# Attention heads taken in pairs on TensorE, with three score banks, five places of exponentials and one more head in flight

## The chip, the cores and the metric

The kernel runs on one core of one Trainium2 chip. The metric is device time in microseconds for one execution of the whole program. TensorE does the matrix products, VectorE (DVE) and ScalarE (ACT) the elementwise work, GpSimd (POOL) and SyncE (SP) issue transfers. Each engine works through its own list of instructions in order, and waits on semaphores that the others raise.

## The reference

Two layers of a decoder trunk, 256 tokens by 1024 channels, float32. Each layer mixes tokens in three branches with 16 heads in all, then runs a SwiGLU.

```
h   = rms_norm(x) * (1 + scale1) + shift1
A: 8 heads, 96 wide queries and keys, dense causal attention
B: 4 heads, 64 wide, own block of 256 keys, ALiBi
C: 4 heads, 64 wide, the 64 keys with the highest indexer score, ALiBi
p   = softmax(q k^T * scale + mask);  y = p v          (each head)
x   = x + gate1 * ((sum_i sigmoid(g_i) * (y_i @ w_br_i)) @ w_out)
x   = x + gate2 * SwiGLU(rms_norm(x) * (1 + scale2) + shift2)
```

For C the keys are chosen by sixteen rounds of "eight largest, then strike them out" on the indexer's scores.

## The kernel before

Products with weights are done in three passes of a split format: each weight slab of 128 x 2048 is loaded by SP into `raw` (three places), copied by ACT into `w_hi` (function `hi`), and its rest is put by DVE into `w_lo` (function `lo`). `lo_ready` tells TensorE that a slab can be used. A ring of three slabs ties the engines together: `hi` of slab n waits until slab n-3 has been used.

The change lies in the stage of the heads. It has one loop on each engine, over n, and each loop runs past the sixteen heads by a few steps so that the work of several heads overlaps. Heads 0 to 3 are branch B, 4 to 11 branch A, 12 to 15 branch C. Each loop sees a head n at a step of its own:

- TensorE, step n: `scores(n+1)` (two products into bank 4 or 5), `turn_p(n-2)` (three transposes of the probabilities into bank 6 or 7), `weigh_v(n-3)` (probabilities times V into one half of the 128 partitions of bank 2 or 3; two heads fill one bank). At steps 1, 3, 5, 8, 10, 12, 15 and 18 (`GATE_STEPS`) half a slab of gate logits follows, 24 products, `gate_slab`.
- DVE, step n: `scores_max(n)` (mask, maximum over keys, negative maximum), `normalize(n-1)`, on odd n from 5 the remainder `y_lo` of a pair of heads, at n = 5, 10, 14 and 20 a `lo` of a weight slab, then one or two rounds of the key selection up to n = 10, and at n = 11 the mask of branch C. In layer 0 an `ada_next` follows at n = 15 and 17.
- ACT, step n: `expo(n)` (two exponentials), the copy of the transposed head n-2 from PSUM into `pt_sb`, on odd n from 5 the copy `y_hi` of a pair from PSUM, and at n = 4, 9, 13 and 19 a `hi` of a weight slab with the tanh of a finished gate slab behind it (`gate_act`).

A pair's chain is thus: `weigh_v` of both heads on TensorE, `y_hi` on ACT, `y_lo` on DVE. `pt_sb` and the buffers in which a head's probabilities lie (`p_sb`) rotate, the latter over four places. The queries of two heads of B or C lie in the two halves of the partitions of `pq_t`; `kz_t` holds the keys of one head in its half and zeros in the other, so that a score product over all 128 rows takes one head alone.

Behind the loop come the branch projections: `branch` of slab `S_BR` (it needs `y_lo` of the first six pairs), `turn_row` twice, then slab `S_BR + 1`, `S_BR + 2` and `S_BR + 3`. `lo(S_BR)` is the one at n = 14 of the DVE loop, `lo(S_BR + 1)` that at n = 20.

Of the kernel before, what the change touches and what calls it, by code (L numbers as in the profile page):

```python
# [10 lines left out]
ACT = mybir.ActivationFunctionType  # L11
# [177 lines left out]

PAIR_Y = [4, 5, 0, 1, 2, 3, 6, 7]  # L190
# [12 lines left out]
def build(nc, x, c, ada, slabs, vec, gain_rows, const, out):  # L203
    with ExitStack() as ctx:
# [53 lines left out]
        p_sb = [acc[:, 384 * i:384 * (i + 1)] for i in range(4)]  # L258
        pt_sb = [acc[:, 2304 + 384 * i:2304 + 384 * (i + 1)] for i in range(2)]
# [248 lines left out]
        def _(pe):  # L508
# [95 lines left out]
            for l in range(DEPTH):  # L604
# [178 lines left out]
                def scores(n):  # L783
                    kind, h = HEADS[n]
                    if kind == "a":
                        q, k = qk_t[0:A_QK, h, :], qk_t[0:A_QK, A_HEADS + h, :]
                    else:
                        j = (0 if kind == "c" else 1)
                        q, k = pq_t[:, 2 * j + h // 2, :], kz_t[:, 4 * j + h, :]
                    if n == 0:  # L790

                        pe.wait_ge(gate_out.sem, gate_out.at(l, 8))
                    if n >= 2:

                        pe.wait_ge(ttr_done.sem, ttr_done.at(l, 2 * (n - 1)))
                    b = bank[4 + n % 2]
                    nc.tensor.matmul(b[:, 0:P], q[:, 0:P], k[:, 0:P], start=True, stop=True)
                    nc.tensor.matmul(b[:, P:P + T], q[:, P:T], k[:, :], start=True, stop=True).then_inc(scored.sem, 1)

                def turn_p(n):  # L800

                    pe.wait_ge(p_ready.sem, p_ready.at(l, n + 1))
                    if n >= 2:

                        pe.wait_ge(pt_out.sem, pt_out.at(l, n - 1))
                    for j in range(3):
# [4 lines left out]
                def weigh_v(n):
                    kind, h = HEADS[n]
                    at = {"a": P * h + A_NOPE, "b": C_BV + HD * h, "c": C_CV + HD * h}[kind]
                    pair = n // 2
                    if n % 2 == 0 and pair >= 2:

                        pe.wait_ge(y_lo_done.sem, y_lo_done.at(l, pair - 1))
                    pe.wait_ge(pt_out.sem, pt_out.at(l, n + 1))
                    r, y = HD * (n % 2), bank[2 + pair % 2]
                    nc.tensor.matmul(y[r:r + HD, 0:T], proj[:, 0, at:at + HD], pt_sb[n % 2][:, 0:T],  # L820
                                     start=True, stop=False, skip_group_check=True)
                    nc.tensor.matmul(y[r:r + HD, P:T], proj[:, 1, at:at + HD],
                                     pt_sb[n % 2][:, T:T + P], start=False, stop=True,
                                     skip_group_check=True).then_inc(pv_done.sem, 1)

                scores(0)
                for n in range(NH + 3):
                    if n + 1 < NH:
                        scores(n + 1)
                    if 2 <= n <= NH + 1:  # L830
                        turn_p(n - 2)
                    if n >= 3:
                        weigh_v(n - 3)
                    if n in GATE_STEPS:
                        half = GATE_STEPS.index(n)
                        gate_slab(l, 8 + half // 2, (half % 2,))

                for hf in range(2):
                    banks = BR_BANKS[hf]

                    def branch(slot, b0, base, k0, n_k):
                        hi, lo = [y_hi[:, k0 + k, :] for k in range(n_k)], [y_lo[:, k0 + k, :] for k in range(n_k)]
                        return channel_slab(slot, [(bank[b0 + m // 2][:, (m % 2) * T:(m % 2 + 1) * T], m * P,
                                                    [base + 512 * k for k in range(n_k)], hi, lo, m % 2 == 0)
                                                   for m in range(4)], True, True)

                    s = S_BR + 2 * hf

                    pe.wait_ge(y_lo_done.sem, y_lo_done.at(l, (B_HEADS + A_HEADS) // 2))
                    if hf:  # L850
                        pe.wait_ge(row_out.sem, row_out.at(l, 2))
                    slot = slab(l, s)
                    branch(slot, banks[0], 0, 0, 4).then_inc(slab_used.sem, 1)
# [112 lines left out]
        def _(act):  # L966
# [88 lines left out]
            for l in range(DEPTH):  # L1055
# [164 lines left out]
                def expo(n):  # L1220
# [3 lines left out]
                    for t, (c0, c1) in enumerate(((0, P), (P, P + T))):  # L1224
                        nc.scalar.activation(p_sb[n % 4][:, c0:c1], p_sb[n % 4][:, c0:c1], ACT.Exp,  # L1225
# [3 lines left out]
                for n in range(NH + 4):  # L1229
                    if n < NH:  # L1230
                        expo(n)
                    if 2 <= n <= NH + 1:
                        act.wait_ge(p_tp.sem, p_tp.at(l, n - 1))
                        if n >= 4:

                            act.wait_ge(pv_done.sem, pv_done.at(l, n - 3))
                        nc.scalar.activation(pt_sb[n % 2], bank[6 + n % 2][:, 0:P + T], ACT.Copy)\
                            .then_inc(pt_out.sem, 1)
                    if n >= 5 and n % 2:
                        pair = (n - 5) // 2  # L1240
                        act.wait_ge(pv_done.sem, pv_done.at(l, 2 * pair + 2))
                        nc.scalar.activation(y_hi[:, PAIR_Y[pair], :], bank[2 + pair % 2][:, 0:T],
                                             ACT.Copy).then_inc(y_hi_done.sem, 1)
# [85 lines left out]
        def _(dve):  # L1329
# [115 lines left out]
            for l in range(DEPTH):  # L1445
# [203 lines left out]
                def scores_max(n):  # L1649
# [4 lines left out]
                    if n >= 4:  # L1654

                        dve.wait_ge(p_tp.sem, p_tp.at(l, n - 3))
                    for t, (c0, c1) in enumerate(((0, P), (P, P + T))):
                        nc.vector.tensor_tensor_reduce(p_sb[n % 4][:, c0:c1], bank[4 + n % 2][:, c0:c1], mask[:, c0:c1],  # L1658
# [6 lines left out]
                def normalize(n):  # L1665
                    dve.wait_ge(exped.sem, exped.at(l, 2 * n + 2))
                    link(nc.vector.reciprocal(rinv[n % 2], rowsum[n % 2]))
                    for t, (c0, c1) in enumerate(((0, P), (P, P + T))):
                        ins = nc.vector.tensor_scalar(p_sb[n % 4][:, c0:c1], p_sb[n % 4][:, c0:c1],
# [3 lines left out]
                for n in range(NH + 5):  # L1673
# [4 lines left out]
                    if 5 <= n < NH + 4 and n % 2:  # L1678
                        pair = (n - 5) // 2
                        dve.wait_ge(y_hi_done.sem, y_hi_done.at(l, pair + 1))  # L1680
                        nc.vector.tensor_tensor(y_lo[:, PAIR_Y[pair], :], bank[2 + pair % 2][:, 0:T],
# [187 lines left out]
```

## Time and profile before

| | us |
|---|---|
| median of 3 runs | 949.47 (948.67 to 950.23) |
| the profiled execution | 948.36 |
| its span, first to last instruction | 946.3 |
| TensorE busy | 900.5 (95%), 5020 instructions |
| DVE busy | 701.9 (74%) |
| ACT busy | 497.6 (53%) |
| mean granted TensorE clock | 0.991 |

TensorE is busy for 95% of the span, but its ends are modelled and its instructions overlap, so the share alone doesn't say that it sets the time of every stage. The stage of the heads runs from about 182 to 246 us in layer 0 and from about 644 to 706 us in layer 1. In the rows an fp32 product stands as two instructions (x2); L797 and L798 are the scores, L807 the transposes, L820 and L822 `weigh_v`, L529 to L531 the products of weight slabs; L1658 and L1662 are `scores_max`, L1667 and L1669 `normalize`, L1681 `y_lo`, L1343 `lo`, L1225 `expo`, L1237 the copy into `pt_sb`, L1242 `y_hi`, L982 `hi`, L1037 `gate_act`.

### The profile page before, as it was taken

Reading aid. Unit: us, or ns where it says so; the run is one execution under the profiler, and the core shown is the slowest. Engines: PE = TensorE matmul, PEld = TensorE weight load, DVE = VectorE, ACT = ScalarE, POOL = GpSimd, SP = SyncE. Lnnn points to the kernel's source line nnn. Section 1 sums busy time; section 2 is a strip of 40 time slices with the busy share of each in tenths; the row PEclk is TensorE's granted clock in tenths of the full one; section 3 lists DMA queues with packets and bytes.
Section 4 is the critical chain, followed back from the end, with each engine's and each line's share of the span. In section 5 each row is a group of like instructions: output and inputs, shape, how many; then the busy total and the mean of one; then the engine's idle time right before and its main releaser. Section 6 shows DMA issues by size and latency. Waiting matters only on the chain.

```text
span 946.3 us, 12773 instructions
## 1 busy us (share of the span) xinstructions
PE 900.5 (95%) x5020; PEld 767.1 (81%) x5020; DVE 701.9 (74%) x1119; ACT 497.6 (53%) x718; POOL 27.7 (3%) x51
## 2 busy tenths in 40 slices
PE   8998988999999999999989998899899999999998
PEld 6788978977887888888868997898689778888886
DVE  5988899787797767586579967987867966575454
ACT  5554965356448443443473469474454664343441
POOL 0010000000000000000001000000000000000000
PEclk9999989999999999999999999999999999999999
DMA  9979723414743857777538973251245456554451
GB/s 377 412 288 398 269 95 134 178 45 169 277 145 145 314 204 271 297 269 277 212 134 330 379 250 142 99 196 63 89 161 195 181 182 220 218 184 184 166 178 45
DMA packets 29582, 198.12 MB, mean 209 GB/s; under 512 B 3282, under 2 KB 3794, under 8 KB 7507
## 3 DMA queue, kind: packets, MB, share of 16 engines
q1 hardware_dynamic: 23474, 155.22, 43.9%
q0 software_dynamic: 5760, 41.95, 11.7%
q8 instruction: 40, 0.66, 0.3%
q10 hardware_dynamic: 288, 0.14, 0.1%
q14 instruction: 20, 0.16, 0.0%
HBM read 196.24 MB, written 1.05 MB: 208 GB/s over the span
## 4 chain that ended last, share of the span: by engine, by line
PE 51%; DVE 31%; ACT 9%; DMA 6%; issue 4%; DVEq 0%; ACTq 0%
PE bank L568 12%; PE bank L570 12%; PE bank L569 12%; DVE w_lo L1343 10%; DMA raw<-in_slabs_dram 5%; PE bank L529 4%; PE bank L531 3%; PE bank L530 3%; ACT w_hi L982 3%; DVE score L1528 2%; DVE front L1350 2%; DVE acc L1658 2%; DVE acc L1350 1%; DVE score L1585 1%; PE bank L917 1%
## 5 line engine op out<-in xcount | busy, mean ns | idle before, releaser
L1343 DVE TENSOR_TENSOR w_lo<-raw,w_hi 128x2048 fp32r<-128x2048 f32 (+2 forms) x146 | 316.5, 2172 | 139.0 <-ACT w_hi L982 137.5
L982 ACT ACTIVATE w_hi<-raw 128x2048 fp32r<-128x2048 f32 (+2 forms) x146 | 264.3, 1811 | 150.7 <-PE bank L570 92.4
L568 PE MATMUL bank<-w_hi,h_hi 128*128 128x512 f32 x536 | 211.3, 394 | 8.2 <-DVE w_lo L1343 5.1
L570 PE MATMUL bank<-w_lo,h_hi 128*128 128x512 f32 x536 | 209.2, 390 | 0.0
L569 PE MATMUL bank<-w_hi,h_lo 128*128 128x512 f32 x536 | 208.9, 390 | 0.0
L568 PEld LDWEIGHTS bank<-w_hi,h_hi 128*128 128x128 f32 x536 | 100.6, 188 | 34.3 <-DVE w_lo L1343 7.7
L529 PE MATMUL bank<-h_hi,w_hi 128*128 128x256 f32 x384 | 113.2, 295 | 10.0 <-DVE w_lo L1343 10.0
L570 PEld LDWEIGHTS bank<-w_lo,h_hi 128*128 128x128 f32 x536 | 100.6, 188 | 21.3
L569 PEld LDWEIGHTS bank<-w_hi,h_lo 128*128 128x128 f32 x536 | 100.7, 188 | 20.1
L530 PE MATMUL bank<-h_lo,w_hi 128*128 128x256 f32 x384 | 110.0, 286 | 0.0
L531 PE MATMUL bank<-h_hi,w_lo 128*128 128x256 f32 x384 | 109.9, 286 | 0.0
L529 PEld LDWEIGHTS bank<-h_hi,w_hi 128*128 128x128 f32 x384 | 74.9, 195 | 14.5 <-DVE w_lo L1343 9.0
L1350 DVE CUSTOM_DVE_ANT_0 front<-front,cond,cols 128x1024 f32<-128x1024 f32 x68 | 84.4, 1279 | 1.9 <-DMA front<-in_ada_dram 1.7
L530 PEld LDWEIGHTS bank<-h_lo,w_hi 128*128 128x128 f32 x384 | 74.9, 195 | 0.1
L531 PEld LDWEIGHTS bank<-h_hi,w_lo 128*128 128x128 f32 x384 | 74.9, 195 | 0.0
L568 PE MATMUL bank<-w_hi,y_hi 128*128 128x512 f32 x176 | 71.3, 405 | 0.0
L569 PE MATMUL bank<-w_hi,y_lo 128*128 128x512 f32 x176 | 69.5, 395 | 0.0
L570 PE MATMUL bank<-w_lo,y_hi 128*128 128x512 f32 x176 | 69.4, 394 | 0.0
L1287 ACT ACTIVATE proj<-bank 128x256 f32<-128x256 f32 x44 | 16.9, 383 | 76.3 <-PE bank L570 76.2
L1225 ACT ACTIVATE acc<-acc,small 128x128 f32<-128x128 f32 x64 | 28.6, 449 | 47.1 <-DVE small L1662 47.1
L570 PEld LDWEIGHTS bank<-w_lo,y_hi 128*128 128x128 f32 x176 | 33.2, 189 | 7.8
L569 PEld LDWEIGHTS bank<-w_hi,y_lo 128*128 128x128 f32 x176 | 33.3, 189 | 6.8
(204 smaller groups left out, 1321.9 us busy)
## 6 DMA issues: line engine op xcount, KB each, us to landing
raw<-in_slabs_dram SPq DMA_DIRECT2D x124, 1024.0 KB, 4.9
front<-in_ada_dram POOLq DMA_DIRECT2D x29, 1024.0 KB, 6.6
acc<-in_ada_dram POOLq DMA_DIRECT2D x11, 1024.0 KB, 8.1
raw<-in_slabs_dram SPq DMA_DIRECT2D x16, 552.0 KB, 7.8
front<-in_ada_dram SPq DMA_DIRECT2D x5, 1024.0 KB, 10.7
raw<-in_slabs_dram SPq DMA_DIRECT2D x6, 768.0 KB, 6.1
proj<-in_ada_dram SPq DMA_DIRECT2D x2, 1024.0 KB, 8.8
x_t<-in_x_dram SPq DMA_DIRECT2D x2, 512.0 KB, 4.4
```

Of the source, the lines that this page charges most:

```text
L529: nc.tensor.matmul(b_out, st_hi, mv_hi, start=start, stop=False, skip_group_check=True)
L530: nc.tensor.matmul(b_out, st_hi, mv_lo, start=False, stop=False, skip_group_check=True)
L531: return nc.tensor.matmul(b_out, st_lo, mv_hi, start=False, stop=stop, skip_group_check=True)
L568: nc.tensor.matmul(o, hh, wh, start=first, stop=False)
L569: nc.tensor.matmul(o, hl, wh, start=False, stop=False)
L570: return nc.tensor.matmul(o, hh, wl, start=False, stop=final)
L982: nc.scalar.activation(w_hi[:, n % RING, 0:w], raw[:, n % RING, 0:w], ACT.Copy).then_inc(hi_ready.sem, 1)
L1225: nc.scalar.activation(p_sb[n % 4][:, c0:c1], p_sb[n % 4][:, c0:c1], ACT.Exp, bias=negmax[n % 2][:, t:t + 1], scale=slope, accum_out=rowsu ...
L1343: nc.vector.tensor_tensor(w_lo[:, n % RING, 0:w], raw[:, n % RING, 0:w], w_hi[:, n % RING, 0:w], ALU.subtract).then_inc(lo_ready.sem, 1)
L1350: ins = nc.vector.tensor_tensor_reduce(w, w, cond[:], 1.0, cols[:, l, col:col + 1], ALU.mult, ALU.add, mod[:, l, col:col + 1])
L1528: ins = nc.vector.scalar_tensor_tensor(out=score[:, c0:c1], in0=relu_b[h % 4][:, c0:c1], scalar=wt, in1=score[:, c0:c1], op0=ALU.mult, op1 ...
L1658: nc.vector.tensor_tensor_reduce(p_sb[n % 4][:, c0:c1], bank[4 + n % 2][:, c0:c1], mask[:, c0:c1], 1.0, NEG, ALU.add, ALU.max, rowmax[n % ...
```

## The change

It touches the stage of the heads on all three engines.

- The scores of B and C are computed for two heads together, `scores_pair`: head e takes 64 rows of `pq_t` and of `kz_t`, and the products of the two heads follow one another in turn into two banks. Those of A stay single.
- Three banks take the scores (4, 5, 3) rather than two; bank 2 alone takes the weighted V.
- `weigh_v` handles a pair: head 0 into partitions 0 to 63, head 1 into 64 to 127, in turn. It stands at odd steps, and waits for `y_lo` of the pair before.
- `p_sb` has five places and `pt_sb` three. `turn_p`, and the copy into `pt_sb`, see head n-3 at step n. `y_hi` and `y_lo` of a pair move from odd steps from 5 to even steps from 6.
- The wait for the last gate tanh moves from the first scores to the first `weigh_v`.
- `branch` of slab `S_BR` moves into the loop, to step 18, behind the gate slab; the last pair's `weigh_v` stands at step 19, behind it.

The core of the diff:

```diff
+SC_BANKS = (4, 5, 3)
-        p_sb = [acc[:, 384 * i:384 * (i + 1)] for i in range(4)]
-        pt_sb = [acc[:, 2304 + 384 * i:2304 + 384 * (i + 1)] for i in range(2)]
+        p_sb = [acc[:, 384 * i:384 * (i + 1)] for i in range(5)]
+        pt_sb = [acc[:, 1920 + 384 * i:1920 + 384 * (i + 1)] for i in range(3)]
...
+                def scores_pair(n):
+                    kind, h = HEADS[n]
+                    if n >= 2:
+                        pe.wait_ge(ttr_done.sem, ttr_done.at(l, 2 * (n - 1)))
+                    j = 0 if kind == "c" else 1
+                    q = pq_t[:, 2 * j + h // 2, :]
+                    at = [slice(HD * e, HD * (e + 1)) for e in range(2)]
+                    b = [bank[SC_BANKS[(n + e) % 3]] for e in range(2)]
+                    for e in range(2):
+                        nc.tensor.matmul(b[e][:, 0:P], q[at[e], 0:P], kz_t[at[e], 4 * j + h + e, 0:P], start=True, stop=True)
+                    for e in range(2):
+                        nc.tensor.matmul(b[e][:, P:P + T], q[at[e], P:T], kz_t[at[e], 4 * j + h + e, :], start=True,
+                                         stop=True).then_inc(scored.sem, 1)
...
+                def weigh_v(pair):
+                    if pair:
+                        pe.wait_ge(y_lo_done.sem, y_lo_done.at(l, pair))
+                    else:
+                        pe.wait_ge(gate_out.sem, gate_out.at(l, 8))
+                    pe.wait_ge(pt_out.sem, pt_out.at(l, 2 * pair + 2))
...
+                    for e in range(2):
+                        nc.tensor.matmul(bank[2][HD * e:HD * (e + 1), 0:T], proj[:, 0, at[e]:at[e] + HD],
+                                         pt_sb[(2 * pair + e) % 3][:, 0:T],
+                                         start=True, stop=False, skip_group_check=True)
+                    for e in range(2):
+                        nc.tensor.matmul(bank[2][HD * e:HD * (e + 1), P:T], proj[:, 1, at[e]:at[e] + HD],
+                                         pt_sb[(2 * pair + e) % 3][:, T:T + P], start=False, stop=True,
+                                         skip_group_check=True).then_inc(pv_done.sem, 1)
...
+                scores_pair(0)
+                for n in range(NH + 4):
                     if n + 1 < NH:
-                        scores(n + 1)
-                    if 2 <= n <= NH + 1:
-                        turn_p(n - 2)
-                    if n >= 3:
-                        weigh_v(n - 3)
+                        if HEADS[n + 1][0] == "a":
+                            scores(n + 1)
+                        elif n % 2:
+                            scores_pair(n + 1)
+                    if 3 <= n <= NH + 2:
+                        turn_p(n - 3)
+                    if n >= 5 and n % 2:
+                        weigh_v((n - 5) // 2)
                     if n in GATE_STEPS:
                         half = GATE_STEPS.index(n)
                         gate_slab(l, 8 + half // 2, (half % 2,))
+                    if n == NH + 2:
+                        first_branch(0)
...
-                for n in range(NH + 4):
+                for n in range(NH + 5):
                     if n < NH:
                         expo(n)
-                    if 2 <= n <= NH + 1:
-                        act.wait_ge(p_tp.sem, p_tp.at(l, n - 1))
-                        if n >= 4:
-                            act.wait_ge(pv_done.sem, pv_done.at(l, n - 3))
-                        nc.scalar.activation(pt_sb[n % 2], bank[6 + n % 2][:, 0:P + T], ACT.Copy)\
+                    if 3 <= n <= NH + 2:
+                        m = n - 3
+                        act.wait_ge(p_tp.sem, p_tp.at(l, m + 1))
+                        if m >= 3:
+                            act.wait_ge(pv_done.sem, pv_done.at(l, m - 2))
+                        nc.scalar.activation(pt_sb[m % 3], bank[6 + m % 2][:, 0:P + T], ACT.Copy)\
                             .then_inc(pt_out.sem, 1)
-                    if n >= 5 and n % 2:
-                        pair = (n - 5) // 2
+                    if n >= 6 and n % 2 == 0:
+                        pair = (n - 6) // 2
                         act.wait_ge(pv_done.sem, pv_done.at(l, 2 * pair + 2))
...
-                    if 5 <= n < NH + 4 and n % 2:
-                        pair = (n - 5) // 2
+                    if n >= 6 and n % 2 == 0:
+                        pair = (n - 6) // 2
                         dve.wait_ge(y_hi_done.sem, y_hi_done.at(l, pair + 1))
```

## Rows read from the trace of the kernel before

**Rows 1.** Windows, layer 0's stage: length, busy PE, PEld, DVE, ACT, POOL, clock, DMA.
```profile
182.00:246.00 64.00, 57.97 (x387) 46.95 (x388) 51.87 (x198) 35.09 (x98) 2.62 (x5) 1.00 0.30 109
```

**Rows 2.** Waits, 182 to 262 us: total us, times, longest.
```profile
DVE y_lo L1681 <- ACT y_hi L1242: 8.1, 7, 1.4
```

**Rows 3.** Timeline of DVE, step 9: start us, duration us, engine, line.
```profile
212.37 0.29 DVE L1658 CUSTOM_DVE_ANT_0 acc<-bank,konst 128x128 f32<-128x128 f32 x1
...
213.04 0.17 DVE L1662 TENSOR_SCALAR small<-small 128x2 f32<-128x2 f32 x1
...
214.91 0.42 DVE L1681 TENSOR_TENSOR y_lo<-bank,y_hi 128x256 fp32r<-128x256 f32 x1 [1.05 <-ACT y_hi L1242]
215.25 0.42 DVE L1584 MAX8 small<-score 128x8 f32<-128x256 f32 x1
...
216.23 0.29 DVE L1658 CUSTOM_DVE_ANT_0 acc<-bank,konst 128x128 f32<-128x128 f32 x1
```

**Rows 4.** Timeline of ACT, steps 9 and 10.
```profile
213.25 0.40 ACT L1225 ACTIVATE acc<-acc,small 128x128 f32<-128x128 f32 x1 [1.03 <-DVE small L1662]
...
214.51 0.37 ACT L1242 ACTIVATE y_hi<-bank 128x256 fp32r<-128x256 f32 x1
214.77 1.91 ACT L982 ACTIVATE w_hi<-raw 128x2048 fp32r<-128x2048 f32 x1
...
217.11 0.40 ACT L1225 ACTIVATE acc<-acc,small 128x128 f32<-128x128 f32 x1
```

**Rows 5.** Timeline of DVE, steps 12 to 16.
```profile
224.68 0.29 DVE L1658 CUSTOM_DVE_ANT_0 acc<-bank,sel_nd 128x128 f32<-128x128 f32 x1
...
226.09 0.28 DVE L1658 CUSTOM_DVE_ANT_0 acc<-bank,sel_nd 128x128 f32<-128x128 f32 x1
...
230.66 2.29 DVE L1343 TENSOR_TENSOR w_lo<-raw,w_hi 128x2048 fp32r<-128x2048 f32 x1
...
232.87 0.28 DVE L1658 CUSTOM_DVE_ANT_0 acc<-bank,sel_nd 128x128 f32<-128x128 f32 x1
...
235.75 1.27 DVE L1350 CUSTOM_DVE_ANT_0 front<-front,cond,cols 128x1024 f32<-128x1024 f32 x1
...
238.16 0.16 DVE L1667 RECIPROCAL small<-small 128x2 f32<-128x2 f32 x1
```

**Rows 6.** Timeline, the stage's first scores and their first reader.
```profile
182.51 0.46 PE L797 MATMUL bank<-kz_t,front 128*128 128x128 f32 x2 [0.78 <-ACT front L1037]
...
183.44 0.29 DVE L1658 CUSTOM_DVE_ANT_0 acc<-bank,konst 128x128 f32<-128x128 f32 x1 [3.25 <-PE bank L798]
```

**Rows 7.** Timeline of PE, the stage's end in layer 0, and `turn_p(15)` in layer 1.
```profile
238.96 0.55 PE L807 MATMUL bank<-konst,acc 128*128 128x128 f32 x3 [1.42 <-DVE acc L1669]
...
240.09 0.65 PE L820 MATMUL bank<-acc,proj 128*64 128x256 f32 x2
...
240.88 0.39 PE L529 MATMUL bank<-h_hi,w_hi 128*128 128x256 f32 x1
...
249.55 1.04 PE L561 MATMUL bank<-konst,row 128*128 128x128 f32 x8
250.34 0.37 PE L529 MATMUL bank<-y_hi,w_hi 128*128 128x256 f32 x1
...
699.14 0.55 PE L807 MATMUL bank<-konst,acc 128*128 128x128 f32 x3
```

**Rows 8.** Timeline of PE, the indexer's products on four row quarters.
```profile
111.57 0.61 PE L735 MATMUL bank<-row,front 32*128 32x256 f32 x8
```

**Rows 9.** Timeline, then windows of PE: length, busy, clock, DMA share, GB/s.
```profile
151.44 0.39 PE L529 MATMUL bank<-h_hi,w_hi 128*128 128x256 f32 x1 [2.27 <-DVE w_lo L1343]
...
153.00:154.00 1.00, 1.00 (x6) 0.50 0.77 311
...
118.00:142.00 24.00, 20.46 (x132) 0.86 0.28 99
142.00:166.00 24.00, 20.12 (x155) 0.93 0.37 132
```

More of the change, by code:

```diff
@@ L807, in turn_p @@
                         last = nc.tensor.transpose(bank[6 + n % 2][:, j * P:(j + 1) * P],
-                                                   p_sb[n % 4][:, j * P:(j + 1) * P], ident)
+                                                   p_sb[n % 5][:, j * P:(j + 1) * P], ident)
                     last.then_inc(p_tp.sem, 1)
[L811 to L824, printed above, removed]
@@ L826, in _ @@
-                scores(0)
-                for n in range(NH + 3):
-                    if n + 1 < NH:
-                        scores(n + 1)
-                    if 2 <= n <= NH + 1:
-                        turn_p(n - 2)
-                    if n >= 3:
-                        weigh_v(n - 3)
+                def weigh_v(pair):
[4 more added lines that the diff above has]
+                    pe.wait_ge(pt_out.sem, pt_out.at(l, 2 * pair + 2))
+                    at = []
+                    for n in (2 * pair, 2 * pair + 1):
+                        kind, h = HEADS[n]
+                        at.append({"a": P * h + A_NOPE, "b": C_BV + HD * h, "c": C_CV + HD * h}[kind])
+                    for e in range(2):
[6 more added lines that the diff above has]
+                                         skip_group_check=True).then_inc(pv_done.sem, 1)
@@ new lines, in branch, with first_branch @@
+                def branch(slot, b0, base, k0, n_k):
+                    hi, lo = [y_hi[:, k0 + k, :] for k in range(n_k)], [y_lo[:, k0 + k, :] for k in range(n_k)]
+                    return channel_slab(slot, [(bank[b0 + m // 2][:, (m % 2) * T:(m % 2 + 1) * T], m * P,
+                                                [base + 512 * k for k in range(n_k)], hi, lo, m % 2 == 0)
+                                               for m in range(4)], True, True)
+                def first_branch(hf):
+                    pe.wait_ge(y_lo_done.sem, y_lo_done.at(l, (B_HEADS + A_HEADS) // 2))
+                    slot = slab(l, S_BR + 2 * hf)
+                    branch(slot, BR_BANKS[hf][0], 0, 0, 4).then_inc(slab_used.sem, 1)
@@ L836, in _ @@
                         gate_slab(l, 8 + half // 2, (half % 2,))
+                    if n == NH + 2:
+                        first_branch(0)
                 for hf in range(2):
                     banks = BR_BANKS[hf]
[L841 to L845, printed above, removed]
                     s = S_BR + 2 * hf
-                    pe.wait_ge(y_lo_done.sem, y_lo_done.at(l, (B_HEADS + A_HEADS) // 2))
                     if hf:
                         pe.wait_ge(row_out.sem, row_out.at(l, 2))
-                    slot = slab(l, s)
-                    branch(slot, banks[0], 0, 0, 4).then_inc(slab_used.sem, 1)
+                        first_branch(1)
                     if hf == 0:
```

32 lines of the change are left out of this document (14 added, 18 removed).

## The prediction

> **What bounds the kernel now.** The page shows TensorE busy for 95% of the span, so at first sight any TensorE work that is saved is time that is saved. The view that decides is that of the stage of the heads. Its window [rows 1] has TensorE busy 57.97 of 64 us and DVE 51.87 of 64. I then read the waits. DVE waits once for scores, at the stage's start [rows 6], and after that for nothing but `y_hi`, 7 times and 8.1 us in all [rows 2]. DVE's timeline is otherwise without a gap from 183.44 to 243 us, and the same in layer 1 up to the last `normalize`. TensorE has some 6 us of gaps in the same stretch, which end with a release by DVE or ACT; the one at 238.96 is such [rows 7]. So in this stage DVE and ACT together set the pace and TensorE follows, nearly full.
>
> The wait of DVE has a form that one step shows [rows 3, 4]. The negative maximum starts at 213.04, ACT's exponentials of the same head at 213.25, its copy into `pt_sb` follows, `y_hi` starts at 214.51, and DVE's `y_lo` at 214.91. That is 1.87 us after the maximum and 1.66 us after the exponentials' start; DVE has only about 0.73 us of its own work to put between (`scores_max` and `normalize` take 1.41 us together, 224.68 to 226.09 [rows 5], 0.68 of which lie ahead of the maximum). `y_lo` itself takes 0.34 (214.91 to 215.25). One `y_lo` thus costs DVE 1.48 us, and it is ACT's order that sets it, not TensorE. Behind the stage TensorE runs without a gap through the branches, so a delay at the stage's end counts in full.
>
> **The change part by part.** I number times on layer 0's clock; layer 1 starts its stage at 645.12 instead of 183.44, 461.68 later, and repeats it.
>
> *TensorE's saving.* A head's `weigh_v` takes 0.79 us (240.09 to 240.88), two of them with the transposes ahead 1.92 (238.96 to 240.88) [rows 7]. Whether halves run side by side, only a near row can say: on row quarters eight instructions of 256 columns took 0.61 us [rows 8], no longer than the two of one `weigh_v`, 0.65 [rows 7]. I take it that halves do so too. A pair's `weigh_v` then costs 0.79 instead of 1.45 (0.66 saved, eight times a layer), and a pair of scores 0.65 less (four times a layer): 7.9 us of TensorE a layer. The other end is nothing saved. The Trainium skill, TensorEngine Tiling (Array Packing), Theoretical Speedup, gives up to 2 times where a dimension is at most 64, which is the saving that I take; the same page, Key Properties, says that a change of tiling mode drains the engine, and it would put more such changes around the paired scores. By either rule only TensorE's slack changes. As DVE never waits for scores in the body, I count this saving at nothing there. It counts in the last two `weigh_v`, which are on the path below.
>
> *The start.* The first scores wait 0.78 us for the tanh of the last gate [rows 6]; that wait moves to the first `weigh_v`, which comes 13 us later. DVE starts 0.83 earlier, at 182.61: gain 0.83 a layer.
>
> *`y_lo` on even steps.* Up to step 9 there are two of them as before, and one with a longer wait of 0.15 becomes a usual one: step 9 of DVE starts at 211.37 instead of 212.37. Now ACT's order matters. At step 9 ACT does expo, copy, then `hi` and the tanh, 2.34 us (214.77 to 217.11 [rows 4]). Before, `y_hi` stood ahead of `hi` in that step. Now it is in step 10, behind it. ACT: expo(9) starts 212.25, expo and copy take 1.26, `hi` and tanh 2.34, expo(10) starts 215.85, so `y_lo` at 215.85 + 1.66 = 217.51. DVE would have been there at 213.75 + 1.41 = 215.16. With `y_lo` 0.34, `lo` 2.21 (230.66 to 232.87 [rows 5]) and a round of selection 0.98 (215.25 to 216.23 [rows 3]), step 11 starts at 221.04.
>
> Step 11 has no `y_lo` now and the mask of C in place of a round of the same length: 3.86 (212.37 to 216.23 [rows 3]) less 1.48, so step 12 starts at 223.42. It was 224.68 [rows 5] with one `y_lo` more behind it; with that 1.48 added we are at 224.9, the 0.83 gone and 0.2 more. Step 12 has a `y_lo` (1.41 + 1.48 = 2.89 with its wait): step 13 at 226.3. Step 13 is 1.41: step 14 at 227.7. ACT: expo(13) 227.17, 1.26 for it and the copy, `hi` and tanh 2.34, expo(14) starts at 230.8, `y_lo` at 232.4. DVE is ready at 229.1, so it stands for 3.3 us; before, this step had no such wait. Then `y_lo` and `lo`: step 15 starts at 234.95, where it started at 232.87 before [rows 5]. This is 2.1 us later than before, 2.9 later than without the two hold-ups.
>
> *A new wait, TensorE for bank 2.* `weigh_v(pair)` waits for `y_lo` of the pair before. Queued behind it are a gate half or the next scores. In the body TensorE has the room (DVE's next scores were issued ahead of it), but its stalls grow: before pair 5 it stands with 0.45 us of transposes between 227.5 and 232.9.
>
> *The end of the stage.* Layer 0: step 15 of DVE ends at 236.36, `ada_next` takes 2.41 (235.75 to 238.16 [rows 5]), `normalize(15)` 0.65, `y_lo` of pair 5 0.34: 239.76. `weigh_v` of pair 6 can't start before (239.85), and `turn_p(15)` stands behind it. Before, `turn_p(15)` started at 238.96, so 0.89 later. In layer 1, without `ada_next`, ACT's two copies and `y_hi` give `y_lo` of pair 5 at 237.86 and `weigh_v` at 238.3; before 699.14 - 461.68 = 237.46, 0.84 later. From there to the first product of slab `S_BR + 1` took 11.38 us (238.96 to 250.34 [rows 7]).
>
> Now: `weigh_v` 0.79, transposes 0.45, gate half and first branch 8.67 (240.88 to 249.55), `weigh_v` of pair 7 0.79, and then the **new chain**. `lo(S_BR + 1)` is in DVE's step 20, behind `y_lo` of pair 7, which waits for `y_hi`, which waits for the `weigh_v` that now comes after the branch. Before, that `lo` was done some 4.6 us ahead of its use. Now it is V's end + 0.11 + 0.40 (`y_hi` to `y_lo`) + 0.34 + 2.21 + 0.05 = 3.1 us, of which `turn_row` covers 0.79 (249.55 to 250.34): TensorE stands for 2.3 us. Sum 13.8 against 11.38: 2.4 later. Together 3.3 in layer 0 and 3.3 in layer 1. The slabs behind it have room: `S_BR + 2` and `S_BR + 3` follow in DVE at once, and their products are due 5.7 us and more later. POOL's waits for the last `weigh_v` let its transfers start some 10 us later, and SP's load of the first `S_OUT` slab some 8 us later; their readers come over 10 us behind, so I count them at nothing, at most 2 us.
>
> *The clock.* An idle stretch of 2.27 us before 151.44 was followed by a granted clock of 0.50 (1.2 instead of 2.4 GHz) from 153 to 154; over 24 us the mean was 0.93, so 24 x 0.07 = 1.7 us were lost [rows 9]. The two other idle stretches of such a length in the trace were followed by the low level too (one of them lies from 118 to 142 us, mean 0.86, 3.4 us lost [rows 9]); those before 238.96 and before `scores`, of 1.4 us and less, were not. The new stall of 2.3 us ahead of `S_BR + 1` is like the first: 1.7 a layer, all on the path. The near-idle stretch before pair 5 costs 1.7 on the gate half that follows: in layer 0 DVE's `ada_next` covers all but 0.15, in layer 1 it delays `turn_p(13)`, ACT's copy, `y_hi` and the bank by 1.7. The bounds are 0 and 3.4 for each. The Trainium skill, TensorE: Matmul & The Clock Gate, says as well that the default state is throttled and that activity releases it; the trace agrees.
>
> *Sum.* Layer 0: 3.3 + 1.7 + 0.15 = 5.2. Layer 1: 3.3 + 1.7 + 1.7 = 6.7. Together **11.8 us slower** (rounded), 948.36 + 11.8 = 960.2 for the profiled execution. That one lies 1.1 below the median of the runs, so the median is forecast at 949.47 + 11.8 = 961.3.
>
> **The rivals.** *The clock stays up.* Then only the chains count, 2 x 3.3 = 6.6: 956.1. Against it stand three idle stretches of this length out of three. *Halves don't run side by side.* The two `weigh_v` on the path cost 1.45 each: 4 x 0.66 = 2.6 more, 963.9. *ACT's hold-ups at steps 10 and 14 do not come about* (`y_hi` isn't reached late, or DVE has other slack). The pace gains 2.9 a layer: 2 x 0.4 = 0.8, and with the clock 3.4 more: 953.7. *TensorE is the bound after all.* The place is the whole stage; the price is 7.9 us saved and 0.83 at the start a layer, against 2.3 for `S_BR + 1`: 2 x 6.4 = 12.8 **faster**, 936.7. It decides from the point at which DVE would be seen to wait for scores; for it speaks the 95%, against it that this wait occurs once a layer. *It does nothing that shows:* the gains at the start and the stall at the end cancel, 949.5.
>
> **How the numbers follow.** Forecast 0.50; clock stays up 0.19; not side by side 0.11; no hold-ups 0.08 (slower still, as 953.7); TensorE bound 0.07; nothing 0.05. The first three hold 0.80. With the bounds of the clock (5 us down, and up by 1.7 for one more drop, with 2.6) the range is 955.0 to 966.0. A measurement of this kernel tells 0.2%, 1.9 us, from no change. Faster 0.07, same 0.05, slower 0.88.
>
> **What would show it.** Right: DVE's waits for `y_hi` include one of over 2 us at step 10, one of over 3 at step 14 and one of some 8 for the last pair; ACT's `w_hi` and tanh stand between two exponentials ahead of it; TensorE waits about 2.3 us for `w_lo` at the first product behind `turn_row`, and for `y_lo` before `weigh_v`; PEclk falls below 1 in the slices of both stages. Scores and `weigh_v` pairs take about half. Wrong: DVE waiting for scores inside the stage, or `lo(S_BR + 1)` done before `turn_row`, would throw the sum over.

## The result and the profile after

| | before | after |
|---|---|---|
| median, us | 949.17 (948.67 to 950.23, 4 runs) | 961.87 (960.78 to 963.63, 4 runs) |
| the profiled execution | 948.36 | 962.44 |
| its span | 946.3 | 960.4 |
| TensorE busy | 900.5 (95%) | 889.7 (93%) |
| DVE busy | 701.9 | 701.7 |
| mean granted TensorE clock | 0.991 | 0.978 |

The ratio after to before is 1.0134 [1.0116, 1.0152]: the kernel with heads in pairs is 1.3% slower. The forecast was 961.3, from 955.0 to 966.0. TensorE does 10.8 us less and the program takes 12.7 us more.

The lines of the code have moved: L793 and L794 are now the single scores, L806 and L808 those of a pair, L818 the transposes, L835 and L839 `weigh_v`, L532 to L534 the products of slabs, L564 `turn_row`, L1684 and L1688 `scores_max`, L1707 `y_lo`, L1369 `lo`, L1250 `expo`, L1268 `y_hi`, L1007 `hi`, L1062 `gate_act`.

The page of the kernel after, its head and its line of the clock by slices:

```profile
span 960.4 us, 12775 instructions
...
PEclk9999999998999999999999999999989999999999
```

Waits of the kernel after, 182 to 270 us (us in total, times, longest), beside [rows 2]:

```profile
DVE y_lo L1707 <- ACT y_hi L1268: 17.7, 7, 8.5
...
PE bank L835 <- DVE y_lo L1707: 8.2, 6, 3.6
ACT w_hi L1007 <- DMA raw<-in_slabs_dram: 7.9, 1, 7.9
...
PE bank L532 <- DVE w_lo L1369: 2.1, 1, 2.1
```

DVE waits for `y_hi` as often as before and more than twice as long. Two rows are new: TensorE waits for `y_lo` before `weigh_v`, and once for a `w_lo`.

Window of layer 0's stage after (length, busy PE, PEld, DVE, ACT, POOL, clock, DMA), beside [rows 1]:

```profile
182.00:246.00 64.00, 49.86 (x371) 42.54 (x370) 49.21 (x196) 33.43 (x96) 1.05 (x2) 0.92 0.25 94
```

TensorE is busy for 8.1 us less of the same 64 us, and its clock is 0.92 where it was 1.00. DVE's busy time is 2.7 us less: both engines stand more. The stage is longer now, so the same 64 us hold a little less of it (371 instructions of TensorE instead of 387).

Timeline of DVE after, the `y_lo` of steps 10 and 14, the next head's maximum, then the last `y_lo` and the `lo` behind it:

```profile
218.01 0.42 DVE L1707 TENSOR_TENSOR y_lo<-bank,y_hi 128x256 fp32r<-128x256 f32 x1 [2.19 <-ACT y_hi L1268]
...
232.88 0.42 DVE L1707 TENSOR_TENSOR y_lo<-bank,y_hi 128x256 fp32r<-128x256 f32 x1 [3.17 <-ACT y_hi L1268]
...
235.42 0.28 DVE L1684 CUSTOM_DVE_ANT_0 acc<-bank,sel_nd 128x128 f32<-128x128 f32 x1
...
252.30 0.42 DVE L1707 TENSOR_TENSOR y_lo<-bank,y_hi 128x256 fp32r<-128x256 f32 x1 [8.52 <-ACT y_hi L1268]
252.64 4.48 DVE L1369 TENSOR_TENSOR w_lo<-raw,w_hi 128x2048 fp32r<-128x2048 f32 x2
```

Timeline of ACT after, in front of the second of these:

```profile
228.57 0.47 ACT L1263 ACTIVATE acc<-bank 128x384 f32<-128x384 f32 x1
228.95 1.90 ACT L1007 ACTIVATE w_hi<-raw 128x2048 fp32r<-128x2048 f32 x1
230.75 0.58 ACT L1062 ACTIVATE front<-bank 128x512 f32<-128x512 f32 x1
231.22 0.39 ACT L1250 ACTIVATE acc<-acc,small 128x128 f32<-128x128 f32 x1
...
232.47 0.37 ACT L1268 ACTIVATE y_hi<-bank 128x256 fp32r<-128x256 f32 x1
```

`w_hi` (1.90) and the tanh (0.58) lie between two heads' exponentials, and `y_hi` comes behind them. DVE has stood since 229.71 for it.

Timeline of PE after, from before pair 5 to slab `S_BR + 1`, beside [rows 7]:

```profile
233.35 1.12 PE L835 MATMUL bank<-acc,proj 128*64 128x256 f32 x4 [3.65 <-DVE y_lo L1707]
...
241.09 0.65 PE L835 MATMUL bank<-acc,proj 128*64 128x256 f32 x4 [0.99 <-DVE y_lo L1707]
241.57 0.39 PE L839 MATMUL bank<-acc,proj 128*64 128x128 f32 x4
241.89 0.55 PE L818 MATMUL bank<-konst,acc 128*128 128x128 f32 x3
...
251.74 1.09 PE L564 MATMUL bank<-konst,row 128*128 128x128 f32 x8
254.97 0.38 PE L532 MATMUL bank<-y_hi,w_hi 128*128 128x256 f32 x1 [2.14 <-DVE w_lo L1369]
```

The same stretch in windows of PE (length, busy PE, clock, DMA share, GB/s):

```profile
230.00:233.00 3.00, 0.00 (x0) 0.73 0.00 0
233.00:236.00 3.00, 2.65 (x13) 0.50 0.01 3
236.00:239.00 3.00, 3.00 (x19) 0.63 0.83 265
251.00:254.00 3.00, 1.83 (x17) 1.00 0.21 33
254.00:257.00 3.00, 2.02 (x10) 0.71 0.94 388
257.00:260.00 3.00, 3.00 (x21) 0.72 0.98 412
260.00:263.00 3.00, 3.00 (x28) 1.00 1.02 431
```

The clock is low from within the idle stretch of 3.65 us on, and low behind the one of 2.14 us, and the work behind both runs on it. Layer 1 differs before pair 5: there the clock falls ahead of the long stretch, which starts at 698.48, behind two waits of 1.91 and 0.92 us, and stays low for 9 us and more:

```profile
692.00:695.00 3.00, 1.41 (x11) 1.00 0.38 161
696.00:705.00 9.00, 5.66 (x28) 0.50 0.05 7
```

### The profile page after: what moved, and what is told of

Same layout as the page of the kernel before. It is cut to its first block, busy times and chain, and to the rows that moved or that the text cites. A ratio compares the mean times of both kernels' runs of the same rounds, so it can differ in the third digit from the quotient of the medians.

```text
span 960.4 us, 12775 instructions
## 1 busy us (share of the span) xinstructions
PE 889.7 (93%) x5020; PEld 761.9 (79%) x5020; DVE 701.7 (73%) x1119; ACT 497.2 (52%) x718; POOL 27.5 (3%) x51
## 3 DMA queue, kind: packets, MB, share of 16 engines
HBM read 196.24 MB, written 1.05 MB: 205 GB/s over the span
## 4 chain that ended last, share of the span: by engine, by line
PE 50%; DVE 31%; ACT 9%; DMA 5%; issue 4%; DVEq 0%; ACTq 0%
PE bank L571 12%; PE bank L573 12%; PE bank L572 12%; DVE w_lo L1369 11%; DMA raw<-in_slabs_dram 5%; PE bank L532 4%; PE bank L533 4%; PE bank L534 4%; DVE score L1554 2%; ACT w_hi L1007 2%; DVE front L1376 2%; DVE acc L1684 2%; DVE score L1611 1%; ACT acc L1250 1%; PE bank L942 1%
## 5 line engine op out<-in xcount | busy, mean ns | idle before, releaser
L1369 DVE TENSOR_TENSOR w_lo<-raw,w_hi 128x2048 fp32r<-128x2048 f32 (+2 forms) x146 | 316.2, 2172 | 130.0 <-ACT w_hi L1007 128.4
L1007 ACT ACTIVATE w_hi<-raw 128x2048 fp32r<-128x2048 f32 (+2 forms) x146 | 264.0, 1810 | 150.9 <-PE bank L573 92.6
L532 PE MATMUL bank<-h_hi,w_hi 128*128 128x256 f32 x384 | 115.5, 301 | 14.3 <-DVE w_lo L1369 14.3
L533 PE MATMUL bank<-h_lo,w_hi 128*128 128x256 f32 x384 | 112.3, 292 | 0.0
L534 PE MATMUL bank<-h_hi,w_lo 128*128 128x256 f32 x384 | 111.9, 292 | 0.0
L532 PEld LDWEIGHTS bank<-h_hi,w_hi 128*128 128x128 f32 x384 | 77.4, 202 | 18.7 <-DVE w_lo L1369 11.4
L533 PEld LDWEIGHTS bank<-h_lo,w_hi 128*128 128x128 f32 x384 | 77.5, 202 | 0.0
L534 PEld LDWEIGHTS bank<-h_hi,w_lo 128*128 128x128 f32 x384 | 77.3, 201 | 0.0
L1250 ACT ACTIVATE acc<-acc,small 128x128 f32<-128x128 f32 x64 | 28.6, 447 | 52.5 <-DVE small L1688 52.5
L532 PE MATMUL bank<-y_hi,w_hi 128*128 128x256 f32 x128 | 37.8, 295 | 4.3 <-DVE w_lo L1369 4.3
## 6 DMA issues: line engine op xcount, KB each, us to landing
front<-in_ada_dram SPq DMA_DIRECT2D x5, 1024.0 KB, 10.8
```

Of the source, the lines that this page charges most:

```text
L532: nc.tensor.matmul(b_out, st_hi, mv_hi, start=start, stop=False, skip_group_check=True)
L533: nc.tensor.matmul(b_out, st_hi, mv_lo, start=False, stop=False, skip_group_check=True)
L534: return nc.tensor.matmul(b_out, st_lo, mv_hi, start=False, stop=stop, skip_group_check=True)
L1007: nc.scalar.activation(w_hi[:, n % RING, 0:w], raw[:, n % RING, 0:w], ACT.Copy).then_inc(hi_ready.sem, 1)
L1250: nc.scalar.activation(p_sb[n % 5][:, c0:c1], p_sb[n % 5][:, c0:c1], ACT.Exp, bias=negmax[n % 2][:, t:t + 1], scale=slope, accum_out=rowsu ...
L1369: nc.vector.tensor_tensor(w_lo[:, n % RING, 0:w], raw[:, n % RING, 0:w], w_hi[:, n % RING, 0:w], ALU.subtract).then_inc(lo_ready.sem, 1)
```

## The experiments

My theory was that of the forecast: the order of ACT and DVE sets the stage's pace, the late `lo(S_BR + 1)` its end, and each standstill costs a drop of the clock besides. The rivals were a TensorE bound and a clock that doesn't matter. For each kernel I read four points in each layer, in us: from DVE's first `scores_max` to that of step 15 (step 15), and to the first product of slab `S_BR + 1` (`S_BR + 1`); from there to the first product of `w_out` (rest); and from the last tanh ahead of the stage to that product (whole). What whole has over the other two together is the start, from the tanh to the first `scores_max`.

The first point needs care. In e2_hi_behind, e4_both, e8_both_br2 and e9_ylo_after_max `lo(S_BR)`, 2.2 us of DVE, stands behind the `scores_max` of step 15, and in the others ahead of it. In e9_ylo_after_max a `y_lo` more stands behind it as well. So 2.2 us of what these four gain at step 15 is only that move; what the pace gains is seen from `S_BR + 1` on.

| kernel | layer 0: step 15, `S_BR + 1`, rest, whole | layer 1 |
|---|---|---|
| before | 49.43, 66.90, 17.36, 85.93 | 49.43, 65.40, 17.36, 84.43 |
| after | 52.28, 71.83, 18.89, 91.57 | 52.29, 71.51, 18.80, 91.16 |
| e1_lo_last | 52.26, 69.78, 18.53, 89.16 | 52.27, 69.52, 18.54, 88.91 |
| e3_fill | 52.27, 71.78, 17.38, 90.01 | 52.26, 71.91, 17.36, 90.12 |
| e2_hi_behind | 47.24, 69.59, 18.89, 89.33 | 46.79, 68.34, 18.90, 88.09 |
| e4_both | 46.79, 65.53, 18.51, 84.89 | 46.79, 65.51, 18.54, 84.90 |
| e7_lo_all | 48.29, 66.89, 18.54, 86.28 | 48.28, 67.01, 18.54, 86.40 |
| e5_tanh_wait | 49.43, 66.91, 17.36, 84.93 | 49.44, 65.41, 17.35, 83.41 |
| e6_two_passes | 50.22, 66.73, 17.35, 85.75 | 49.20, 64.75, 17.36, 83.78 |
| e8_both_br2 | 46.82, 66.04, 17.36, 84.25 | 47.13, 64.35, 17.35, 82.55 |
| e9_ylo_after_max | 41.39, 63.08, 17.36, 81.29 | 43.87, 62.57, 17.35, 80.76 |
| e10_before_ylo | 47.08, 63.43, 17.35, 81.43 | 47.07, 63.06, 17.35, 81.07 |

### e1_lo_last: the late `lo` alone

```diff
 # DVE, step 20, kernel after
+                    if n == 20:
+                        lo(l, S_BR + 1)
                     if n >= 6 and n % 2 == 0:
                         ... y_lo of the pair
-                    if n - 2 in GATE_AT:
+                    if n - 2 in GATE_AT and n < 20:
                         ... lo
```

> The changed kernel with one move: in DVE's step 20 the remainder of slab S_BR + 1 (lo) is made ahead of y_lo of the last pair, not behind it. Theory (the tail's new chain V, y_hi, y_lo, lo holds TensorE for 2.1 us a layer, and the idle stretch brings the low clock, 1.7 us more): TensorE's wait behind turn_row vanishes, the clock stays up there, 2 x 3.8 = 7.7 us faster than the changed kernel, about 954.2. Rival (the wait is a symptom, the slab would be late anyway through its hi or its transfer): the wait stays, 961.9. Rival on the clock (the stall costs only itself): 2 x 2.1 = 4.3 faster, 957.6.

Measured: 956.54 (956.08 to 958.17), ratio to before 1.008 [1.0065, 1.0095], 5.3 less than after. Slab `S_BR + 1` comes 2.05 and 1.99 us sooner, and the clock in the window from 246 to 275 us rose from 0.94 to 1.00. But the rest fell only from 18.8 to 18.5, as a wait took the place of the low clock. Waits of this kernel from 182 to 275 us:

```profile
PE bank L532 <- DVE proj L1750: 1.1, 1, 1.1
```

L1750 adds up the three branches' results, into `proj`: DVE is now late with that. The stall and its drop of the clock go together here, and a part of what they give back is used up by what is late next. The time lies between the two values expected, 954.2 and 957.6.

### e3_fill: the idle stretch filled, the wait left

Five products, whose result in bank 6 nobody reads, run while TensorE would stand.

```diff
                             turn_row(l, 0, half, bank[half])
+                        for _ in range(5):
+                            nc.tensor.matmul(bank[6][:, 0:T], kz_t[:, 0, 0:P], kz_t[:, 0, :], start=True, stop=True)
```

> The changed kernel with five products of 256 columns, whose result nobody reads, put on TensorE behind turn_row in the place of the 2.1 us in which it stands for w_lo of slab S_BR + 1. The chain to w_lo is untouched. Theory (the idle stretch brings the clock down and that costs 1.7 us a layer by itself): the first product of the slab starts as late as now, within 0.2 us, but the clock stays at its upper level behind it, 3.4 us faster, about 958.5. Rival (the low clock comes from elsewhere or costs nothing on the path): 961.9, or a little more.

Measured: 958.97 (957.02 to 963.19), 1.0108 [1.0079, 1.0137]. Timeline of PE:

```profile
254.82 2.32 PE L885 MATMUL bank<-kz_t 128*128 128x256 f32 x10
257.13 0.39 PE L532 MATMUL bank<-y_hi,w_hi 128*128 128x256 f32 x1
257.36 0.28 PE L533 MATMUL bank<-y_lo,w_hi 128*128 128x256 f32 x1
257.48 0.28 PE L534 MATMUL bank<-y_hi,w_lo 128*128 128x256 f32 x1
```

The slab starts as late as in after, but its products then start 0.12 us apart, where after has 0.21 behind this stall. The rest is 17.38 and 17.36, which is before's 17.36; so the drop of the clock cost 1.5 us in layer 0 and 1.4 in layer 1. The median fell by 2.9, with an interval of some 3 us to either side. The load of the first `w_out` slab, for which ACT waits 8.8 us here (7.9 in after), costs nothing of the rest.

### e2_hi_behind: `hi` and tanh behind `y_hi`

```diff
-                    if n - 1 in GATE_AT:
-                        hi(l, gate_slab_no(GATE_AT[n - 1]) + 2)
-                        gate_act(l, GATE_AT[n - 1])
+                    if n in HI_STEPS:            # {4: 8, 10: 9, 14: 10, 19: 11}, behind y_hi
+                        hi(l, gate_slab_no(HI_STEPS[n]) + 2)
+                        gate_act(l, HI_STEPS[n])
```

DVE's `lo` stands one step behind each.

> The changed kernel with ACT's hi and tanh of steps 9 and 13 put into steps 10 and 14, behind y_hi, and DVE's lo one step later with them. Theory (hi and tanh ahead of y_hi make DVE stand 1.1 us too long at step 10 and 2.1 at step 14, and TensorE's long stretch before pair 5 brings the low clock): DVE's longest wait for y_hi in the body falls from 3.2 to about 1.1 us, TensorE's 3.6 us stretch to under 2 and the clock stays up on the gate half; 3.2 us of the chain and 0.7 to 1.7 of the clock a layer, about 8 us faster, 954. The tail's stall of 2.1 us stays. Rival (the body's hold-ups are slack, the tail alone costs): under 2 us faster, 960 to 962.

Measured: 954.7 (953.09 to 957.25), 1.0051 [1.0026, 1.0077]. Step 15 comes 5.0 and 5.5 us sooner than in after, but 2.2 us of that is `lo(S_BR)`, which now stands behind it. Timeline of DVE:

```profile
229.18 0.28 DVE L1686 CUSTOM_DVE_ANT_0 acc<-bank,sel_nd 128x128 f32<-128x128 f32 x1
...
230.64 2.29 DVE L1371 TENSOR_TENSOR w_lo<-raw,w_hi 128x2048 fp32r<-128x2048 f32 x1
```

The longest wait of TensorE for `y_lo` falls from 3.6 to 1.2, and the stall at the tail stays. Waits, 182 to 275 us:

```profile
PE bank L837 <- DVE y_lo L1709: 3.7, 5, 1.2
...
PE bank L534 <- DVE w_lo L1371: 2.1, 1, 2.1
```

`S_BR + 1` comes 2.2 and 3.2 us sooner, and that is the gain. The place of `hi` is thus shown to set the pace of the heads. The clock didn't stay up as expected: it was 0.91 from 182 to 226 us and 0.76 from 226 to 246 us (0.96 and 0.83 in after), though no wait for `y_lo` was over 1.2 us.

### e4_both: the two mends together

> Both moves together: ACT's hi and tanh behind y_hi at steps 10 and 14, and the remainder of slab S_BR + 1 ahead of the last y_lo. Theory (two independent costs): the gains add up, 7.7 and 8 us, about 946, which is 3 us faster than the kernel before; what stays of the change is the earlier start, 0.8 us a layer, and an end that is 0.7 us a layer shorter. Rival (the two overlap, one hides the other): 950 or more.

Measured: 949.10 (946.72 to 951.53, 10 runs), 0.9999 [0.9987, 1.0011]. The gains add up: 5.3 and 7.2 alone make 12.5, together they are 12.8. By the stages of the profiled executions they more than add up: 4.7 and 5.3 us alone, 12.9 together. The clock has a part in that: from 226 to 246 us it is 0.91 here and 0.76 in e2_hi_behind. All of the loss is gone, and no more: the time is 3 us over the 946 expected, with the same wait of 1.1 us for `proj` as in e1_lo_last.

### e7_lo_all: every `lo` ahead of its `y_lo`

```diff
+                    if n - 2 in GATE_AT:
+                        lo(l, gate_slab_no(GATE_AT[n - 2]) + 2)
                     if n >= 6 and n % 2 == 0:
                         ... y_lo of the pair
-                    if n - 2 in GATE_AT:
-                        lo(l, gate_slab_no(GATE_AT[n - 2]) + 2)
```

> The changed kernel with lo ahead of y_lo in all of DVE's steps 10, 14 and 20, ACT untouched. DVE then makes the slab's remainder while it would stand for y_hi. Theory: 2.1 us of DVE's chain saved at step 10 and 2.1 at step 14 (the wait is covered by 2.2 us of work), plus the tail's 2.1 and 1.7; TensorE's stretch before pair 5 stays over 2 us, since y_hi stays behind hi and tanh, so the low clock stays there. 6.8 to 8 us a layer, 946 to 948. Rival (the hold-ups are slack): as the move of the last lo alone.

Measured: 953.67 (951.08 to 954.44, 9 runs), 1.0035 [1.0024, 1.0047], some 6 us over what I expected. Step 15 came 4 us sooner, as expected, and the clock still falls, also as expected (0.91 from 226 to 246 us). What failed is what I counted on behind it: the wait for `proj` is there as in e1_lo_last, and `S_BR + 1` comes only 4.9 and 4.5 us sooner, where the last `lo` alone gives 2.0. `y_lo` now waits for the `lo`. That of step 14 starts 1.8 us sooner than in after, not 4, and TensorE still stands before pair 5:

```profile
PE bank L835 <- DVE y_lo L1711: 8.4, 6, 3.9
```

To fill DVE's wait is not to shorten TensorE's.

### e5_tanh_wait: the start alone, in the kernel before

The wait for the last gate tanh moves from TensorE's first scores to its first `weigh_v`; all else is as before.

> The kernel before with one part of the change: the wait for the last gate tanh moves from the first scores to the first weigh_v. Theory (DVE and ACT set the pace, so a start 0.8 us earlier moves the whole chain): 0.8 us a layer, 1.6 us faster than before, about 947.6. Rival (TensorE is the bound, its list is as long as before, the gap only moves behind): no more than 0.3 faster.

Measured: 946.45 (945.51 to 949.11, 6 runs), 0.9968 [0.9955, 0.998], beside 949.62 for before on that chip. The stages are 1.0 us shorter each, all of it at the start: from the tanh to the first maximum it takes 0.66 us, where before has 1.67 and after 0.85. Timeline:

```profile
182.21 0.60 ACT L1036 ACTIVATE front<-bank 128x512 f32<-128x512 f32 x1 [4.13 <-PE bank L531]
...
182.87 0.29 DVE L1657 CUSTOM_DVE_ANT_0 acc<-bank,konst 128x128 f32<-128x128 f32 x1 [2.23 <-PE bank L795]
```

This part of the change is a gain by itself; the medians differ by 3.2, of which the traces place 2.0.

### e6_two_passes: TensorE lightened, in the kernel before

The gate slabs 8 to 11 leave out the product with `w_lo`, the third pass, so their logits are less precise. It takes 64 products of 0.12 us, 7.7 us, from TensorE in each stage, and nothing from DVE or ACT.

> The kernel before; the gate slabs 8 to 11, the ones spread over the stage of the heads, leave out the third pass (rest of the weight times the activation's high part), so that their gate logits are less exact. This takes 8 of 24 products from each of 8 halves, 0.96 us each, 7.7 us of TensorE a layer out of the stage. Theory (DVE and ACT set the pace there): only the last half, behind the last transposes, is on the path, 1 us a layer, so 2 us faster than before, 947, and TensorE's gaps in the stage grow by some 6 us a layer; with gaps over 2 us the low clock may take back up to 1.7 a layer. Rival (TensorE is the bound): 2 x 7.7 = 15 us faster, 934.

Measured: 946.05 (945.69 to 946.53), 0.9961 [0.9948, 0.9974]. 15.4 us of TensorE's work gave 3.6 us by the medians, and of that the traces place 0.8 in the two stages, which are 0.2 and 0.7 shorter; where the other 2.8 us arise isn't shown. The rival of the TensorE bound expected 934, and falls. Windows of this kernel (columns as in [rows 1]):

```profile
182.00:226.00 44.00, 38.18 (x225) 29.28 (x224) 36.41 (x158) 21.85 (x69) 1.05 (x2) 0.92 0.25 96
226.00:246.00 20.00, 17.28 (x109) 13.79 (x108) 16.22 (x42) 13.25 (x29) 1.58 (x3) 0.91 0.34 124
```

Part of what is taken from TensorE comes back as a lower clock, 0.92 and 0.91, where [rows 1] has 1.00: behind a wait of 3.1 us for DVE that ends at 203.19 us it is 0.50 for at least the 4 us from 206 to 210. So this run does not measure what lighter work would give at a full clock.

### e8_both_br2: slab `S_BR + 2` sooner as well

`hi` and `lo` of `S_BR + 2` stand ahead of the last `y_hi` and `y_lo`, on top of e4_both.

> The kernel with both moves (hi and tanh behind y_hi, the remainder of S_BR + 1 ahead of the last y_lo), and hi and lo of slab S_BR + 2 now also ahead of the last pair's y_hi and y_lo. In the run with both moves TensorE waits 1.1 us a layer for m_done at the second half's slab, since DVE's merges begin later. Theory (the two remainders behind the last y_lo are what delays the merges): that wait goes, 1.1 to 1.2 us a layer, 2.3 us faster than the 949.1 with both moves, about 946.8. Rival (hi of S_BR + 3 and its transfer set the merges): no change, 949.

Measured: 947.37 (945.31 to 948.93, 9 runs; a tenth took 1741.82 and isn't explained), 0.9976 [0.9966, 0.9985]. The wait for `proj` is gone and the rest is 17.36 again. With these faults mended the change isn't shown to be worth more than its start alone: e5_tanh_wait has 0.9968 [0.9955, 0.998]. By the stages of the profiled executions it is 0.7 and 0.9 us shorter than e5_tanh_wait; the medians don't show that.

### e9_ylo_after_max: `y_lo` behind the next maximum

In e8_both_br2 DVE still waits for `y_hi` 15 times in the two stages, 18.7 us in all. Here DVE does `scores_max` of the next head first, on top of e8_both_br2.

```diff
                     if n < NH:
                         scores_max(n)
+                    if n >= 7 and n % 2 == 1:
+                        ... y_lo of pair (n - 7) // 2
```

> As the last one, and y_lo of a pair is moved on DVE from behind normalize of an even step to behind scores_max of the next odd step, so that scores_max and normalize (1.4 us) lie in what was the wait for y_hi. Theory (DVE with its 1.05 us wait per pair sets the pace, and the paired products left TensorE room): 5 pairs x 1.05 us a layer come off the chain, 10 us faster than the last one, about 937; where TensorE's gaps stay over 2 us the low clock takes back up to 1.7 a layer, 940. Rival (TensorE or ACT is as near to the bound as DVE): under 4 us faster, 943 or more.

Measured: 940.42 (937.95 to 942.67), 0.9896 [0.9876, 0.9916]; 7.0 less than e8_both_br2 by the move of one operation. DVE's waits for `y_hi` are down from 18.7 to 9.5 us in the two stages; in layer 0 they are 3.7 us, 2.2 of it for the last pair. Window, 182 to 226 us:

```profile
182.00:226.00 44.00, 39.74 (x296) 33.76 (x294) 39.44 (x178) 25.43 (x81) 1.05 (x2) 0.92 0.30 117
```

### e10_before_ylo: the same move without the pairs

e5_tanh_wait with `y_lo` behind the next `scores_max`, `n >= 6` and even there. Heads are single, as before.

> The kernel before, with single heads on TensorE, and two moves: the wait for the last gate tanh sits at the first weigh_v, and y_lo of a pair sits on DVE behind scores_max of the next step. Theory (without the pairs TensorE has only some 4 us of gaps a layer to give): 3 to 4 us a layer faster than the 946.5 with the first move alone, then TensorE is the bound of the stage, 939 to 941, so the pairs are worth about 3 us once DVE is out of the way. Rival (the pairs are worth nothing): as fast as its paired counterpart, within 1 us. Rival (TensorE is already the bound in the kernel before): no gain over 946.5.

Measured: 940.95 (940.01 to 941.39), 0.9909 [0.9894, 0.9924]. Single heads and pairs lie 0.5 us apart, within their intervals: the 3 us that I expected of the pairs are not there, and the rival that they are worth nothing held. Its window from 182 to 226 us, and a row of DVE's timeline:

```profile
182.00:226.00 44.00, 42.99 (x286) 34.84 (x286) 38.81 (x172) 25.70 (x78) 1.05 (x2) 1.00 0.25 97
```

```profile
223.46 0.29 DVE L1657 CUSTOM_DVE_ANT_0 acc<-bank,sel_nd 128x128 f32<-128x128 f32 x1 [1.88 <-PE bank L795]
```

Here TensorE is full, 42.99 of 44 us, and for the first time DVE waits for scores inside the stage. It is the place where the pairs' saving ought to pay. It doesn't: with pairs TensorE is busy for 39.74 of the 44 us at a clock of 0.92. What they save stands as idle time, and the clock falls: TensorE waits 2.3 us for ACT's copy before the first `weigh_v`, and later up to 2.5 us in layer 0 and 3.3 in layer 1 for `y_lo`. Whether pairs would win at a full clock, or with a second bank for the weighted V, wasn't tried.

## Why the prediction was right, step by step

- **The bound.** DVE and ACT set the pace, not TensorE: shown by e2_hi_behind (only ACT's and DVE's order changed, `S_BR + 1` is 2.2 and 3.2 us sooner) and by e6_two_passes (only TensorE's work changed, `S_BR + 1` within 0.7 us), the latter at a lower clock.
- **Side by side.** A pair's `weigh_v` takes 0.80 us (241.09 to 241.89); the sum had 0.79, the rival 1.45. The Trainium skill, TensorEngine Tiling (Array Packing), Theoretical Speedup, gives up to 2 times for such a half, and the row agrees: 1.45 us of work in 0.80. The two scores of a pair take 0.49 and 0.60 us (at 182.19 and 182.51), no longer than one head's.
- **The start.** From the tanh to DVE's first maximum 0.85 instead of 1.67: 0.82 gained in each layer, 0.83 forecast.
- **A wait that the forecast left out.** The first `weigh_v` needs two heads' copies now. In layer 0 TensorE stands 2.32 us for them, up to 196.24 us, and the clock is low from 197.24 to 200.66; layer 1 is alike. It moved nothing on DVE's chain: step 9 starts 28.79 us after the first maximum, and the working had 28.76.
- **The hold-ups.** DVE stood 2.19 us at step 10 and 3.17 at step 14; the working had 2.35 and 3.3. Step 15 starts 52.28 us after the first maximum; the working had 234.95 less 182.61, 52.34.
- **Pair 6.** The working had its `weigh_v` 57.24 us behind the first maximum in layer 0 and 55.69 in layer 1, without the clock. It came at 57.95 and 57.61 (709.16 less 651.55): 0.7 and 1.9 later. The clock term before pair 5 was 0.15 and 1.7. This is the term that was mis-sized, in layer 0: I had `ada_next` cover all but 0.15 of the slow gate half. But the transposes queued behind it started at 239.28, ACT's copy of them stands ahead of the `y_hi` of pair 5, and DVE waited another 0.63 us for that (`y_lo` at 240.61).
- **The tail.** 13.88 us from that `weigh_v` to slab `S_BR + 1` (241.09 to 254.97), 13.8 forecast, with a stall of 2.14 for `w_lo` (2.3 forecast). The drop behind it cost 1.5 and 1.4 (1.7 forecast), as e3_fill shows.
- **Counted at nothing.** The transfers that start later: in after ACT waits 7.87 us for one and the rest doesn't grow by it. That holds.
- **The sum.** The stages grew by 5.64 and 6.73 us; forecast 5.2 and 6.7. Outside them the profiled execution has 1.7 us more: 0.5 ahead of the first stage and 1.1 between the two. No cause is shown for it; in code that no run changed, the tanh ahead of the first stage starts anywhere from 180.52 (e6_two_passes) to 184.50 us (e3_fill). The medians differ by 12.7, the forecast by 11.8. That the median came within 0.6 us of the forecast is closer than the runs agree among themselves, and so partly luck; the stages are the better test.
- **The price of `hi` ahead of `y_hi`.** It was counted as 2.9 us a layer; undone it gave back 2.2 and 3.2 at `S_BR + 1`.
- **The clock.** The rival of a clock that stays up is ruled out in the tail by e3_fill. But the forecast's grounds, that the drops stand behind idle stretches of 2.27 us and more and that those of 1.4 us and less had none, were too simple. Before has another drop, from 589.04 us on, behind a wait of 1.42 us that ends at 588.81, and after has a wait of 2.94 us, up to 150.69 us, behind which the clock stays up for the next 9 us.
- **What I had not seen.** The forecast took before's own wait of DVE for `y_hi` [rows 2] as given. It could be had: moving `y_lo` gave 7.0 us with pairs and 5.5 without (e10_before_ylo less e5_tanh_wait).

## What to carry to other kernels

When a stage is paced by a round of waits between three engines, find the operation at the head of an engine's list that waits while work behind it is ready, and move it behind that work: here one such move gave 7 us where 10.8 us of saved TensorE work gave nothing. When an operation is moved by a step, look at what stands ahead of it in its new place, and at who needs the buffer that it frees. When a change makes TensorE stand, read the granted clock behind the stall as well as the stall, since a drop can cost as much again (1.4 to 1.5 us behind 2.14 us here); and when the stall is gone look for what is late next. When a point in a loop comes sooner, check that no work was merely moved behind it.

## What was not expected of the hardware

Lighter work on TensorE went with a lower clock. In all nine kernels that did less on TensorE in the stage, the granted clock of the window from 182 to 226 us was 0.91 to 0.96: 0.96 in after, 0.92 in e6_two_passes and in e9_ylo_after_max. In the three that did as much as before (before, e5_tanh_wait, e10_before_ylo) it was 1.00, with TensorE busy for 42.99 of 44 us in e10_before_ylo.

The length of one wait doesn't tell whether the clock falls. Drops stand behind single waits of 2.1 to 3.7 us (after, e6_two_passes), but also behind waits of 1.91 and 0.92 us (after, layer 1), of 1.22 us (e6_two_passes, 0.50 from 232.00 us on) and of 1.42 us (before, at 588.81). Behind the wait of 2.94 us in after, which ends at 150.69 us, the clock stayed up until 159.70. What else decides it isn't shown here.

Ten product instructions of no use in an idle stretch (e3_fill) made the stretch behind it shorter than leaving it idle, by 1.4 to 1.5 us in each layer.
